# Part of the memory's key projection placed ahead of a feed-forward, in a two-block fp32 kernel on one Trainium2 core

## The reference, cut to what matters

```python
def second_block(x, mem, ...):
    h = rms_norm(x, pre_mix_g[l]); z = h @ w_in[l]          # gate, attention and convolution branches
    ...
    x = x + rms_norm(y, post_mix_g[l])
    m = rms_norm(mem, mem_g[l])                              # (256, 1024)
    x = x + rms_norm(memory_cross_attention(h, m, w_xq[l], w_xkv[l], w_xo[l]), post_x_g[l])

def memory_cross_attention(h, m, w_q, w_kv, w_o):
    k, v = jnp.split(m @ w_kv, 2, axis=-1)                   # keys: the first 1024 columns of w_kv
    ...
```

## Time and profile before

| | |
|---|---|
| median of 3 runs | 794.24 us (794.18 to 794.38) |
| the profiled execution | 793.84 us |
| its span, first to last instruction | 792.4 us |
| mean granted TensorE clock | 0.999 |
| busy: PE, PEld, DVE, ACT, POOL | 98%, 85%, 72%, 55%, 11% |
| matmuls | 4516 |
| chain that ended last, by engine | PE 91%, DVE 3% |
| HBM | 161.81 MB read, 206 GB/s over the span |

### The profile page before, as it was taken

The page is one execution under the profiler, slowest core; times in us unless marked ns, Lnnn a source line. Parts: engine busy times, 40 slices in busy tenths (PEclk is TensorE's granted clock), DMA queues, the critical chain, the costliest instruction groups (busy, mean ns, idle before and its releaser), DMA issues.

```text
span 792.4 us, 11548 instructions
## 1 busy us (share of the span) xinstructions
PE 777.2 (98%) x4516; PEld 675.1 (85%) x4516; DVE 574.1 (72%) x782; ACT 432.9 (55%) x644; POOL 86.9 (11%) x141
## 2 busy tenths in 40 slices
PE   6999999999999999999999999999999999999997
PEld 5999877788788888888899998889988988888885
DVE  5986999769577676777677989857556666655664
ACT  5554567663555744454465478457645644444452
POOL 5033980000100000000020000011001100000001
PEclk9999999999999999999999999999999999999999
DMA  9999988755546585855556544546433655555551
GB/s 325 367 290 310 365 283 296 276 172 188 172 153 220 178 297 188 282 198 184 181 165 219 181 145 135 174 159 210 145 99 107 217 197 195 188 187 189 198 171 54
DMA packets 83605, 163.61 MB, mean 206 GB/s; under 512 B 5456, under 2 KB 13840, under 8 KB 83552
## 3 DMA queue, kind: packets, MB, share of 16 engines
q1 hardware_dynamic: 81632, 157.31, 58.7%
q10 hardware_dynamic: 1424, 4.81, 1.8%
q0 software_dynamic: 496, 0.76, 0.5%
HBM read 161.81 MB, written 1.05 MB: 206 GB/s over the span
## 4 chain that ended last, share of the span: by engine, by line
PE 91%; DVE 3%; issue 2%; ACT 1%; DMA 1%; SPq 1%; POOL 1%; DVEq 0%; POOLq 0%; ACTq 0%
PE bank L1831 20%; PE bank L1833 19%; PE bank L1832 19%; PE bank L1896 13%; PE bank L1899 7%; PE bank L1844 2%; PE bank L1850 2%; PE bank L1846 2%; DVE ada_acc L1023 1%; DMA raw_ring<-in_w_in 1%; PE bank L1938 1%; PE bank L2496 1%; PE bank L2090 1%; SPq L486 1%; DVE lo_ring L993 1%
## 5 line engine op out<-in xcount | busy, mean ns | idle before, releaser
L993 DVE TENSOR_TENSOR lo_ring<-raw_ring,hi_ring 128x1024 fp32r<-128x1024 f32 x248 | 305.3, 1237 | 147.1 <-ACT hi_ring L532 146.4
L532 ACT CAST hi_ring<-raw_ring 128x1024 fp32r<-128x1024 f32 x248 | 259.3, 1051 | 254.1 <-PE bank L1833 150.4
L1831 PE MATMUL bank<-hi_ring,branch_hi 128*128 128x512 f32 x352 | 139.1, 395 | 0.0
L1832 PE MATMUL bank<-lo_ring,branch_hi 128*128 128x512 f32 x352 | 137.2, 390 | 0.0
L1833 PE MATMUL bank<-hi_ring,branch_lo 128*128 128x512 f32 x352 | 137.1, 389 | 0.0
L1896 PE MATMUL bank<-h_hi_lo,hi_ring 128*128 128x512 f32 x448 | 111.8, 392 | 0.0
L1896 PEld LDWEIGHTS bank<-h_hi_lo,hi_ring 128*128 128x128 f32 x448 | 81.3, 189 | 15.0
L1833 PEld LDWEIGHTS bank<-hi_ring,branch_lo 128*128 128x128 f32 x352 | 66.1, 188 | 14.0
L1831 PEld LDWEIGHTS bank<-hi_ring,branch_hi 128*128 128x128 f32 x352 | 66.1, 188 | 13.8 <-issue 0.7
L1832 PEld LDWEIGHTS bank<-lo_ring,branch_hi 128*128 128x128 f32 x352 | 66.2, 188 | 13.4 <-issue 0.5
L1831 PE MATMUL bank<-h_hi_lo,hi_ring 128*128 128x256 f32 x240 | 69.2, 288 | 0.0
(11 more groups left out here) (293 smaller groups left out, 1182.3 us busy)
## 6 DMA issues: line engine op xcount, KB each, us to landing
raw_ring<-in_w_ff SPq DMA_DIRECT2D x128, 512.0 KB, 3.5
raw_ring<-in_w_in SPq DMA_DIRECT2D x64, 512.0 KB, 4.7
raw_ring<-in_w_out SPq DMA_DIRECT2D x16, 512.0 KB, 3.3
raw_ring<-in_w_xkv SPq DMA_DIRECT2D x16, 512.0 KB, 3.5
mem_v<-in_w_ada SPq DMA_DIRECT2D x12, 512.0 KB, 5.4
mem_k<-in_w_ada SPq DMA_DIRECT2D x12, 512.0 KB, 5.7
ada_ring<-in_w_ada SPq DMA_DIRECT2D x8, 512.0 KB, 6.2
raw_ring<-in_w_branch SPq DMA_DIRECT2D x8, 512.0 KB, 3.2
```

Of the source, the lines that this page charges most:

```text
L532: act.copy(m.hi[:, m.slot(u)], m.raw[:, m.slot(u)]).then_inc(s.hi_done, 1)
L993: dve.tensor_tensor(m.lo[:, m.slot(u)], m.raw[:, m.slot(u)], as_f32(m.hi[:, m.slot(u)]), ALU.subtract).then_inc(s.lo_done, 1)
L1831: pe.matmul(out, a_hi, b_hi, start=start, stop=False, skip_group_check=True)
L1832: pe.matmul(out, a_hi, b_lo, start=False, stop=False, skip_group_check=True)
```

## The change

The keys' columns 512 to 767 are made ahead of the first feed-forward, as two tall units of 512 rows by 256 columns (MEM_KE, units 60 and 61; FF1 is 62 now). Columns 768 to 1023 stay at MEM_K1 as two tall units in place of four; the count of units stays 248. The tall units replace the filler matmuls: one ahead of each token half's turns. The memory is loaded at step 13 of the gate slabs, into `mix` in place of `gates`. ScalarE squares it at steps 17 and 18 and scales it at 19 and 20. TensorE turns it behind the second and third unit of the output projection, with the gain's high and low parts beside that. ScalarE's and VectorE's `after` calls around the turn move: the high and low part of unit 61 come ahead of the first square and scaling. `follow` has 22 steps, with the convolution's norm at 14, 15 and 16 in place of 15, 16 and 18. The taps are spread anew (5 beside each unit of Q2 and K2). In the second attention one copy by ScalarE takes both turned banks, where VectorE took one. The late loads of the adaptive gate use three buffers in place of four, since `mem_k_hi`'s second half is now in use.

```diff
-BRANCH, OUT, FF1 = 44, 52, 60
-MEM_K0, GLU2, Q2, K2, MEM_K1, GELU2, V2, MEM_V0 = 124, 128, 132, 136, 140, 144, 148, 152
+BRANCH, OUT, MEM_KE, FF1 = 44, 52, 60, 62
+MEM_K0, GLU2, Q2, K2, MEM_K1, GELU2, V2, MEM_V0 = 126, 130, 134, 138, 142, 144, 148, 152
...
+    def tall(w, c0):
+        return [w[bass.ds(j * 2 * UK * P, 2 * UK * P), bass.ds(c0, S)].rearrange("(k p) n -> p k n", p=P) for j in range(2)]
...
+    units += tall(w_xkv, UN)
     units += feed_forward(t["w_ff1"][0], t["w_ff2"][0])
...
-    units += slab(w_xkv, UN) + slab(w_in2, 0) + slab(w_in2, 1536) + slab(w_xkv, 2 * UN)
+    units += tall(w_xkv, UN + S) + slab(w_in2, 0) + slab(w_in2, 1536) + slab(w_xkv, 2 * UN)
...
@@ ScalarE, gate slabs, output projection and turn @@
                 act.copy(m.br_hi[:, 6:8, :], m.conv_y1).then_inc(s.mixers_hi, 1)
+                act.dma_start(m.mem, t["mem_2"][0].rearrange("(a p) d -> p a d", p=P)).then_inc(s.mem_in, DMA)
+            if i in (17, 18):
+                if i == 17:
+                    act.wait_ge(s.mem_in, DMA)
+                square_sum(s.mem, i - 17, m.mem)
+            if i in (19, 20):
+                scale_rows(s.mem, i - 19, m.mem, m.mem)
...
         after(OUT + j)
+        if j in (1, 2):
+            gain_hi(s.mem, cols[:, G_MEM:G_MEM + KD], m.memT_hi, range(2 * j - 2, 2 * j))
...
     after(OUT + RING)
+    after(OUT + RING + 1)
     act.wait_ge(s.ff_cols, 2)
     act.wait_ge(*s.post1.x.at(1))
     square_sum(s.ff1t, 0, m.x)
-    after(OUT + RING + 1)
     act.wait_ge(s.used, OUT + 2 * RING)
     post_square(s.post1, 1, 1, OUT_BANKS[1][1])
     after(OUT + RING + 2)
     act.wait_ge(*s.post1.x.at(2))
     square_sum(s.ff1t, 1, m.x)
-    after(FF1 - 1)
+    after(OUT + RING + 3)
+    after(MEM_KE)
     shifted_hi(s.ff1t)
+    after(MEM_KE + 1)
+    act.copy(pair(m.mem_k_hi, 4), bank[2][:, :]).then_inc(s.mem_keys_hi, 1)
...
@@ VectorE @@
+    def keys_lo(n, k):
+        dve.wait_ge(s.mem_keys_hi, n + 1)
+        dve.tensor_tensor(pair(m.mem_k_lo, k), bank[2][:, :], as_f32(pair(m.mem_k_hi, k)), ALU.subtract).then_inc(s.mem_keys, 1)
...
                 post_scale(s.post1, 0, tt, OUT_BANKS[0][tt], m.rows[:, 0, :])
         if j == 1:
             merged_lo(1)
+        if j in (2, 3):
+            gain_lo(s.mem, cols[:, G_MEM:G_MEM + KD], m.memT_hi, m.memT_lo, range(2 * j - 4, 2 * j - 2))
...
     after(OUT + RING)
+    after(OUT + RING + 1)
     scale_rows(s.ff1t, 0, m.x)
     post_scale(s.post1, 1, 1, OUT_BANKS[1][1], m.rows[:, 0, :])
     post_add(s.post1, 1, D)
-    after(OUT + RING + 1)
+    after(OUT + RING + 2)
     scale_rows(s.ff1t, 1, m.x)
...
         if k == KD // 2:
-            after(OUT + RING + 2)
+            after(OUT + RING + 3)
     shifted_lo(s.ff1t, KD - 1)
-    after(FF1 - 1)
+    after(MEM_KE)
+    keys_lo(0, 4)
+    after(MEM_KE + 1)
...
-        conv_taps(5 - j % 2)
+        conv_taps(5)
...
@@ TensorE @@
+    def tall_features(u, j, x_hi, x_lo, b):
+        pe.wait_ge(s.lo_done, u + 1)
+        hi, lo = m.tall(m.hi, u), m.tall(m.lo, u)
+        for k in range(2 * UK):
+            for f in range(2):
+                fc = slice(f * P, f * P + P)
+                mm = three_passes(bank[b][:, f * S:f * S + S], hi[:, k, fc], lo[:, k, fc], x_hi[:, 2 * UK * j + k, :],
+                                  x_lo[:, 2 * UK * j + k, :], j == 0 and k == 0 and f == 0, j == 1 and k == 2 * UK - 1)
+        mm.then_inc(s.used, 1)
...
-    def turn_normed(turn, idle=0):
+    def turn_normed(turn, ahead=None):
         claim(4, 5, 6, 7)
         for tt in range(NT):
-            if tt:
-                keep_busy(idle)
+            if ahead:
+                ahead(tt)
...
+        if j in (1, 2):
+            claim(2 * j + 2, 2 * j + 3)
+            pe.wait_ge(*s.mem.normed.at(NT))
+            for tt in range(NT):
+                transposes(s.mem, m.mem, tt, range(4 * j - 4, 4 * j))
+            free[2 * j + 2], free[2 * j + 3] = s.mem.lo.at(4 * j - 2), s.mem.lo.at(4 * j)
...
+    def early_keys(tt):
+        if tt == 0:
+            claim(2)
+            pe.wait_ge(*s.mem.lo.at(KD))
+        tall_features(MEM_KE + tt, tt, m.memT_hi, m.memT_lo, 2)
+        if tt:
+            free[2] = s.mem_keys, 1
...
-    turn_normed(s.ff1t, idle=16)
+    turn_normed(s.ff1t, early_keys)
...
-    memory_slab(MEM_K1, 1, 2, follow)
+    claim(2)
+    for j in range(2):
+        tall_features(MEM_K1 + j, j, m.memT_hi, m.memT_lo, 2)
+        if j:
+            free[2] = s.mem_keys, 4
+        follow(j)
```

More of the change, by code:

```diff
@@ L426, in slot, with tall @@
         return u % RING
+    def tall(self, ring, u):
+        return ring[:, u % RING].rearrange("p k n -> p (k n)").rearrange("p (k n) -> p k n", n=S)
     def chunk_ps(self, k):
@@ L477, in load @@
             sp.wait_ge(s.lo_done, u - (RING - 1))
-        sp.dma_start(m.raw[:, m.slot(u)], units[u]).then_inc(s.raw_in[m.slot(u)], DMA)
+        tall = MEM_KE <= u < FF1 or MEM_K1 <= u < GELU2
+        sp.dma_start(m.tall(m.raw, u) if tall else m.raw[:, m.slot(u)], units[u]).then_inc(s.raw_in[m.slot(u)], DMA)
     def load_ada(a):
@@ L879, in act_program @@
     for j in range(RING):
+        if j == 0:
+            act.wait_ge(s.used, MEM_K1 + 2)
+            act.copy(pair(m.mem_k_hi, 6), bank[2][:, :]).then_inc(s.mem_keys_hi, 1)
         if j == RING - 1:
@@ L885, in act_program @@
         after(GELU2 + j)
-        follow(RING + j)
+        follow(2 + j)
     for j in range(RING):
@@ L889, in act_program @@
             take_half(V2 + RING, 2, m.v_tok[:, 0, :], s.v2_out)
-            take_turned(s.att2, 2, pair_bank(2), m.turned2[2])
+        after(V2 + j)
+        follow(6 + j)
+    for j in range(RING):
+        if j == 1:
+            take_both(s.att2, 2, pair_bank(2), m.turned2[2])
             normalize(s.att2, 3, m.soft2[3])
-        after(V2 + j)
-        follow(2 * RING + j)
-    for j in range(RING):
         if j == RING - 1:
@@ L897, in act_program @@
         after(MEM_V0 + j)
-        follow(3 * RING + j)
+        follow(10 + j)
     for i, (n, k) in enumerate(OUT2_ORDER):
@@ L902, in act_program @@
         after(OUT2 + i)
-        follow(4 * RING + i)
+        follow(14 + i)
     def squares(turn, post):
@@ L2268, in turn_memory @@
             free[0], free[1] = (s.ff_row, 1), (s.ff_row, 3)
-        if step in (1, 3) and q == 1:
-            pe.wait_ge(*s.ff1.taken.at(2 * step + 2))
-            pe.wait_ge(*s.mem.normed.at(NT))
-            for tt in range(NT):
-                transposes(s.mem, m.mem, tt, range(2 * step - 2, 2 * step + 2), m.mem_ps)
-            free[2], free[3] = s.mem.lo.at(2 * step), s.mem.lo.at(2 * step + 2)
     def feed_forward(f, t, post, beside=None):
@@ L2418, in follow @@
             gate_mix()
+        if step == 14:
+            conv_center()
         if step == 15:
-            conv_center()
+            conv_norm()
         if step == 16:
-            conv_norm()
-        if step == 18:
             conv_silu()
-    memory_slab(MEM_K1, 1, 2, follow)
+    claim(2)
+    for j in range(2):
+        tall_features(MEM_K1 + j, j, m.memT_hi, m.memT_lo, 2)
+        if j:
+            free[2] = s.mem_keys, 4
+        follow(j)
     claim(0, 1)
```

107 lines of the change are left out of this document (39 added, 68 removed).

## The result

| | before | after |
|---|---|---|
| median | 794.28 us (7 executions) | 796.55 us (7 executions, 796.27 to 798.66) |
| ratio | | 1.0033, interval 1.0022 to 1.0044 |
| profiled execution, its span | 793.84, 792.4 us | 796.27, 794.8 us |
| matmuls | 4516 | 4500 |

One of the seven executions of the kernel before took 2739.72 us, the others 794.18 to 794.53; the ratio leaves it out. The changed kernel is slower, by 2.3 us of the medians and by 0.33% of the ratio. The predicted time was 794.7, with 791.6 to 797.2 as the range: the range holds the result. But the prediction took 1.6 us as the limit of no change, to which it gave 0.56, and 2.3 is more; a slower kernel had 0.18. A new run of the same kernel later gave 796.70 (ratio 1.0030, interval 1.0018 to 1.0041).

A forecast was written before the change was run, and what follows sets the result against it. TensorE, busy nearly the whole span, was taken as the bound. -5.76 + 2.4 + 1.15 + 0.5 + 2.2 + 0 = +0.5 us gave 794.7 us as the median, range 791.6 to 797.2.

The forecast's parts named there:

- What leaves TensorE: Keys' second half after the feed-forward: two units of 256-column matmuls fewer, 5.76 us less; the memory's turning gains nothing.
- Step A: Gate slabs: ScalarE's memory squares and scaling delay normalising and the turned probabilities' copy; TensorE waits 0.45 and 1.9, together 2.4 us.
- Step B: End of first output half: four memory low parts on VectorE delay the next unit's low part; TensorE waits 1.15 us.
- Step C: Turn ahead of the feed-forward: tall unit 1 ends after the unchanged chain, so half 1 turns 0.5 us later.
- Step D: Ring of four units at the feed-forward: low parts late for second and third unit, 1.0 and 1.2 lost, 2.2 us.
- Step E: Second block: two steps fewer, VectorE's extra taps up to 1.6 later to first scores; taken as 0, bounds 0 and 1.2.
- Filler becomes work and the rest hides: Rival: the other engines' new work hides, only the turn's cost is paid: -5.3, 788.9 us; chance 0.10.
- The late memory: Rival: the memory's load lands late in the gate slabs, halfway at 154.1, costing 2.9: 797.6 us; chance 0.10.
- The fourth: Rival: Step E at its upper bound together with Step A or Step D at theirs: +2.6, 796.8 us; chance 0.08.

The follow-up runs named there:

- e2: Changed kernel, but VectorE makes the memory's last four low parts behind the second output half's fourth-unit low part: 795.55 us held, median 797.06.
- e6: Changed kernel, but each early tall unit of keys does 6 matmuls in place of 24 (keys partly wrong): no execution held, median 797.52 us.
- e9: Changed kernel, but the feed-forward's low parts come sooner, inside and behind VectorE's shift loop, none ahead of the second scaling: 794.80 us held, median 796.24.
- e12: e10, but VectorE's low part that ran beside GpSimd's power comes two steps later, behind the multiplication with the scales: 789.41 us.
- e4: Changed kernel, but TensorE claims banks 2 and 3 only ahead of the second unit of the second output projection: 794.65 us held, median 794.66.
- e1: Changed kernel, but ScalarE squares both memory rows in step 17 and scales them in the branch units: 794.51 us held, median 794.70.
- e3: Changed kernel, but the feed-forward's second unit's high and low parts come ahead of the turn's second square and scaling, later low parts moved up: 794.99 us held, median 795.99.
- e5: Changed kernel, but the convolution's scales, silu and split come one step later: 798.65 us held (one execution), median 799.89.
- e11: Changed kernel, but 6 unread filler matmuls stand between claiming banks 0, 1 and banks 2, 3 ahead of the second output projection: 796.68 us.
- e10: Changed kernel with the four moves of e1, e2, e9 and e4 together: 789.51 us, ratio 0.9940 to the kernel before.
- e8: Changed kernel with the moves of e1, e2, e9, e4 and e5 together: 791.63 us held, median 791.74.

## Why the prediction was right in its range and wrong in one step

**What leaves TensorE** (-5.76): right. The memory's turns cost 1.74 in the first stretch and give 1.74 back in the second: 5.51 is 2.32 (A) + 1.0 (B) + 0.45 (C) + 1.74, and 0.26 is 2.01 (D) - 1.74.

**Step A**, forecast 2.4 with 0.45 and 1.9: the profile shows 0.40 and 1.92 beyond the pitch, and taking its cause away gave 2.1. Right in place, cause and size.

**Step B**, forecast 1.15: 1.0 by the profile and 1.0 by e2. Right.

**Step C**, forecast 0.5: the size is right (the feed-forward starts 8.46 behind the last output matmul at 220.45, where before it started 8.01 behind), the cause is half of it. The step said that tall unit 1 ends later than the chain, which is as long as before. The first is so, by 0.05 (e6). But the chain itself is 0.46 longer than before (6.79 against 6.33 from the last output matmul to the turns of half 1), so without tall units the turn would be as late. GpSimd's line ahead of the power for half 1's output took 0.66 where it took 0.27 before (216.68):

```profile
221.80 0.66 POOL L1675 TENSOR_SCALAR stat<-stat 128x1 f32<-128x1 f32 x1 [0.26 <-ACT gates L595]
```

It ran beside VectorE's scaling (221.57 to 222.32). That 0.39 was read, not tested.

**Step D**, forecast 2.2 with 1.0 and 1.2: 0.92 and 1.09. Right, and e9 gave 1.8 back.

**Step E**, forecast 0 with bounds 0 and 1.2: this is the step that failed. It took 2.42. The step followed VectorE's taps and the scores and asked whether the probabilities came too late; that part held, there is no wait from the keys to the mix. It did not ask where each piece of side work stands when two of its steps are taken away. The gate's mix came to stand right ahead of a claim of the bank that it writes, 1.9, and the convolution's scales came a step closer behind the power, 0.56 beyond the pitch, of which 0.47 went when nothing was waited for (e12). The 1.95 of e4 and this 0.47 are 2.42, as the windows have it. The upper bound was too low for the same reason: it was built from the taps alone.

With E at 2.4 the sum is -5.76 + 2.4 + 1.15 + 0.5 + 2.2 + 2.4 = +2.9, the result is +2.43. So the sign and nearly the size would have followed from the other steps. That the range held all the same is luck: its upper part, to 797.2, was there for a memory that lands late, and that did not happen. With E's own upper bound of 1.2 the forecast reaches 795.9 only.

**The rivals.** Filler becomes work and the rest hides: half of it is true, the early keys' work on TensorE is free (e6), the other engines' work was not. The late memory: false. It was issued at 135.81, earlier than the 138 of the working, and landed in 8.3 us, at 144.1, 5 us ahead of its use:

```profile
mix<-in_mem ACTq DMA_DIRECT2D x1, 1024.0 KB, 8.3
```

The fourth, 796.8, is near the result in number alone: it wanted A or D at its upper bound, where they stayed at the forecast, and E at 1.2 by the taps.

**What the change is worth.** The idea is sound: with the order mended, the same early keys give 789.5, 4.8 below the kernel before. As it stands, 8.2 us of new waits (A to E) eat 5.76.

## What to carry to other kernels

When steps are taken out of a schedule written by hand, list for every piece of side work what it stood beside before and what it stands beside now, claims of accumulator banks among them; the piece that loses its cover is rarely the one that was edited. Work put into a queue cost nothing here by its amount and everything by its place: four moves of existing instructions made +2.3 into -4.8. Where single executions lie in two groups, compare within a group, or an edit that gains 1 us looks like a loss.

## What was not expected of the hardware

**A wait of 2 us can cost 3.5.** Behind gaps of 1.9 to 2.2 us TensorE's granted clock fell in some executions to a mean of 0.57 or 0.58 over 4 us, for the most part to its lower level of 1.2 GHz from 2.4: matmuls of 512 columns were 0.43 apart in place of 0.23. In that stretch of e1 it is 8 of them, 1.6 us, which is the distance of the two groups (794.51 and 796.14). Between the gap and the fall lay four matmuls at the full rate in e1, and one in e3. In every profiled execution that fell (e1, e2, e3, e5, e6, e9, e11 and the second run of after) each fall stands behind one of the gaps. The clock fell in 26 of the 57 executions of after, e1, e2, e3 and e9, which have the gap ahead of the second output projection, in 2 of 16 where it is closed or filled (e4, e11), and in none of 10 where the gap in the gate slabs is closed too (e10, e12). e5, e6 and e8, which have a gap of 2.1 to 3.0 elsewhere, fell in 4 of 5, 5 of 5 and 2 of 6. e11's one fall at the other gap shows that filling one gap does not end the falls; that closing both does rests on 10 executions, and on the 69 of the kernel before beside the experiments, whose longest wait past the start is 0.95 and none of which fell. Why the share differs so much between kernels with the same gap (3 of 14 for after, 6 of 9 for e2) stays open; the runs were on several chips.

**VectorE holds GpSimd up.** GpSimd's small instruction took 0.19 or 0.20 alone, and 0.98 and 1.03 beside VectorE's low part, ending within 0.06 of it both times (228.78 and 228.73; 512.81 and 512.75); taking the low part away brought 0.20 back (e12). The Trainium skill, SBUF — State Buffer, section Who interferes with whom, states it as a rule: a VectorE instruction with two inputs in SBUF contends with a GpSimd instruction that reads SBUF, and the second to come is blocked until the first has ended. The traces here agree with it. A power of one column on GpSimd stands in this kernel's chain four times around the turn, so what VectorE does meanwhile is part of the chain.
